# A hand-ordered decoder layer: four stage joins rearranged (squares and tables, GLA to NSA, the first decode batch, the output weights)

## The chip, the cores and the metric

One core of a Trainium2 chip runs the whole program. The time is device microseconds of one execution. The kernel before was timed in three runs, and one more execution of it was profiled.

## The reference

One decoder layer in fp32 works on 512 prompt tokens and on 32 sample tokens (8 sequences of 4 new tokens, each behind 4,096 cached ones), with D = 1024 and the same weights for both groups. Cut to what matters:

```python
mod = silu(c) @ w_ada + b_ada                    # six modulation vectors
u = x * (1 + sc1) + sh1                          # x: LayerNorm of the input
z = u @ w_in                                     # split into GLA and NSA columns
o_g = gated linear attention(q_g, k_g, v_g, a_g) # 4 heads, chunks of 64, RMSNorm, swish gate
o_n = nsa(q_n, kv_c, kv_s, kv_w, gates)          # 8 heads, 2 kv heads
x = LN(ALPHA * x + ga1 * (concat(o_g, o_n) @ w_o))
x = LN(ALPHA * x + ga2 * ((silu(gate) * up) @ w_ffn_out))   # gate, up from w_ffn_in
```

NSA sums three attentions with sigmoid gates. One goes over compressed keys and values: every 32 tokens, with a stride of 16, go through a small MLP (`cmp_w1`, gelu, `cmp_w2`). One goes over the 16 blocks of 64 tokens with the highest scores, and one over a window of 512 tokens. For the sample group, the cached rows of the compress branch, of the selected branch and of the window come from HBM.

## The kernel before, in words

The program is written by hand: each of the five engines (PE = TensorE, DVE = VectorE, ACT = ScalarE, POOL = GpSimd, SP, which only issues transfers) has one list of instructions, in the order of the text, and named semaphores join the lists. No scheduler moves anything. An engine that waits holds up everything behind the wait on its list.

The stages, with their times in the profile: LayerNorm and the modulation weights (0 to 50 us); the input projection (50 to 216); GLA (216 to 288); the NSA prompt loop of 32 tiles (288 to 386); eight decode batches, one for each sample sequence (386 to 658); output projection and LayerNorm (658 to 757); the feed-forward part and the last LayerNorm (757 to the end).

Large buffers are shared by the stages. `ring` (the profile's ringreg) has four slots of 1 MB, through which all weights pass, and in decode the selected rows. `RC` (creg) holds U early on, and the compress rows of the even decode batches; `RS` (sreg) holds the squares early on and the compress rows of the odd batches. `Z` (zreg) holds the projection, `XC` and `MIXT` (mixreg) the centred rows and later the attention outputs.

**Head.** DVE writes the centred rows of the LayerNorm (L1907). ACT squares them (`ln_act`, L1514), PE sums the squares. Ahead of the squares ACT waits for all constant tables (`consts_in`), among them the page table `ptc`. PE multiplies the tiles of `w_ada` as they come; tiles 5 to 8 are asked for by SP (L393) as PE frees slots (`weights_used`). DVE waits for the tables ahead of `fold_gain`.

**GLA to NSA.** DVE scales the GLA outputs, first the sample's and then four banks (L2142, L2144). PE transposes heads 0, 2, 1, 3 into banks 4, 5, 0, 1 (L1089) and then the sample's (L1093). DVE multiplies each by its gate into MIXT (L2149, L2152) and then copies the swapped keys (`kswap`, L2162), and POOL copies the swapped queries (L636). PE waits for all of that and computes `scores(0)` into banks of the first two transposes. The loop of 32 tiles then runs on all engines. DVE makes the scaled sample queries zS (L2193) ahead of the loop; the transfers of SP that copy them wait for that.

**Decode batches.** For one batch POOL gathers eight pieces of compress rows (`cmp_load`, L646, 0.5 MB each, into RC or RS) and the selected rows (`slc_load`, L652, 4 MB, into ring). DVE transposes the pieces (`turn_in`, L2199) and the selected keys (L2229). POOL adds pairs (`pair_sums_of`, L667), PE multiplies pieces and sums by `cmp_w1` (`outer`, `inner`), DVE adds the hidden rows up (`hidden_in`, L2236 to L2239), ACT and POOL compute the gelu (`gelu_cubic` L672, `gelu_product` L677), PE makes the compressed keys (`cmp_keys`) and values (`cmp_values`) from it. Then come scores, importance, choice of blocks (DVE, L2257 on), masks, exponentials and values. Each batch's last steps run under the next batch's first. Batch 0 has a code path of its own in many places: `weight_sum(1)` (POOL, L658) prepares the second weight sum that `cmp_w1` needs, and `cmp_load(1)` is issued in two groups of four among batch 0's pair sums.

**Output weights.** SP, in its order, loads the window rows and two pieces of VX for each batch (L458 to L460), then waits until the last batch's values and scores have left the ring, and asks for the four tiles of `w_o` (L382). PE runs `wo_tile(n, h)` (eight column tiles, n, and two halves of the tokens, h), with pieces of the last batch (`cmp_values(7)` and its tail) between them. The late modulation weights (`ada_load`, L469) follow into the slots that the output tiles free.

## Time and profile before

| | |
|---|---|
| three runs | 1202.77, 1206.3, 1208.32 us (median 1206.3) |
| profiled execution | 1201.1 us, its span 1199.3 us |
| mean granted TensorE clock | 0.963 of full speed |
| PE busy | 1123.1 us, 94% of the span |
| DVE busy | 690.5 us, 58% |
| ACT busy | 332.5 us, 28% |
| POOL busy | 304.8 us, 25% |
| HBM read, written | 158.84 MB, 9.24 MB |

The busy time of an engine is an average over stages with different limits, so the places that count are found in the timeline. A timeline row has the start of an instruction or of a run of equal ones, its length, the engine, the line and operation, output <- inputs, shapes, how many, and in brackets the idle time before it with what ended it. A count of x4 with one length means that four instructions took that length together.

### The profile page before, as it was taken

Reading aid. Unit: us, or ns where it says so; the run is one execution under the profiler, and the core shown is the slowest. Engines: PE = TensorE matmul, PEld = TensorE weight load, DVE = VectorE, ACT = ScalarE, POOL = GpSimd, SP = SyncE. Lnnn points to the kernel's source line nnn. Section 1 sums busy time; section 2 is a strip of 40 time slices with the busy share of each in tenths; the row PEclk is TensorE's granted clock in tenths of the full one; section 3 lists DMA queues with packets and bytes.
Section 4 is the critical chain, followed back from the end, with each engine's and each line's share of the span. In section 5 each row is a group of like instructions: output and inputs, shape, how many; then the busy total and the mean of one; then the engine's idle time right before and its main releaser. Section 6 shows DMA issues by size and latency. Waiting matters only on the chain.

```text
span 1199.3 us, 19658 instructions
## 1 busy us (share of the span) xinstructions
PE 1123.1 (94%) x7798; PEld 885.4 (74%) x7798; DVE 690.5 (58%) x1496; ACT 332.5 (28%) x783; POOL 304.8 (25%) x346
## 2 busy tenths in 40 slices
PE   5899999877999799999999899999999999999995
PEld 3577777654677577877777686788887888778884
DVE  2753332688777478877775446554455454563245
ACT  2111110624665244544454213221111111000005
POOL 7200000163535677666662001000010000000000
PEclk8899999877999899999999999999999999999998
DMA  7733332155400776666663316121221221320202
GB/s 292 281 141 140 146 153 94 36 196 141 119 2 8 292 298 277 248 249 258 238 246 141 141 37 241 60 84 71 94 81 70 75 99 48 145 90 12 93 1 75
DMA packets 36842, 165.33 MB, mean 138 GB/s; under 512 B 4968, under 2 KB 15816, under 8 KB 27608
## 3 DMA queue, kind: packets, MB, share of 16 engines
q1 hardware_dynamic: 25304, 94.78, 21.5%
q0 software_dynamic: 11312, 69.38, 14.9%
q8 instruction: 56, 0.92, 0.3%
q14 instruction: 26, 0.21, 0.1%
q10 hardware_dynamic: 144, 0.04, 0.0%
HBM read 158.84 MB, written 9.24 MB: 140 GB/s over the span
## 4 chain that ended last, share of the span: by engine, by line
PE 83%; DVE 6%; DMA 4%; ACT 2%; POOL 2%; issue 1%; SPq 0%; ACTq 0%; DVEq 0%; POOLq 0%
PE PS L366 82%; DMA VX<-out_dram 2%; DMA ptc<-in_ptab_dram 1%; PE PS L1182 1%; POOL ptc L519 1%; ACT trunk L1829 1%; DVE w L2407 1%; DMA ringreg<-in_w_ada_dram 1%; DVE sreg L2455 1%; DVE sreg L2090 0%; DVE creg L2090 0%; PE PS L1255 0%; ACT ringreg L1643 0%; DMA ringreg<-in_w_o_dram 0%; DVE ringreg L2115 0%
## 5 line engine op out<-in xcount | busy, mean ns | idle before, releaser
L366 PE MATMUL PS<-mixreg,w 128*128 128x272 f32 (+1 forms) x596 | 139.7, 386 | 9.9 <-DVE mixreg L2085 4.2
L366 PE MATMUL PS<-creg,ringreg 128*128 128x272 f32 (+1 forms) x564 | 144.2, 400 | 3.5 <-ACT creg L1522 2.8
L366 PE MATMUL PS<-mixreg,ringreg 128*128 128x272 f32 (+1 forms) x532 | 132.3, 402 | 5.5 <-DMA ringreg<-in_w_o_dram 4.4
L366 PEld LDWEIGHTS PS<-mixreg,w 128*128 128x128 f32 x596 | 110.5, 195 | 32.0 <-issue 8.3
L366 PEld LDWEIGHTS PS<-creg,ringreg 128*128 128x128 f32 (+1 forms) x564 | 104.6, 188 | 33.1 <-issue 9.8
L366 PEld LDWEIGHTS PS<-mixreg,ringreg 128*128 128x128 f32 (+1 forms) x532 | 100.2, 191 | 28.0 <-DMA ringreg<-in_w_o_dram 4.8
L366 PE MATMUL PS<-zreg 128*32 128x128 f32 (+4 forms) x832 | 107.2, 327 | 9.1 <-POOL zreg L667 4.8
L366 PE MATMUL PS<-creg,w 128*128 128x256 f32 (+1 forms) x432 | 106.7, 392 | 0.0
L366 PEld LDWEIGHTS PS<-creg,w 128*128 128x128 f32 x432 | 81.8, 193 | 17.6 <-issue 4.3
L366 PEld LDWEIGHTS PS<-zreg 128*32 128x32 f32 (+2 forms) x832 | 73.0, 142 | 23.0 <-issue 6.0
L366 PE MATMUL PS<-mixreg,sreg 128*128 128x272 f32 x352 | 87.3, 395 | 0.0
L366 PEld LDWEIGHTS PS<-mixreg,sreg 128*128 128x128 f32 x352 | 66.1, 190 | 13.1 <-issue 0.2
L366 PE MATMUL PS<-sreg,w 128*128 128x256 f32 x256 | 61.6, 386 | 0.0
L366 PE MATMUL PS<-sreg,ringreg 128*128 128x128 f32 (+2 forms) x488 | 55.2, 309 | 1.3 <-DVE sreg L2096 0.7
L366 PEld LDWEIGHTS PS<-sreg,ringreg 128*128 128x128 f32 (+2 forms) x488 | 46.9, 189 | 11.5 <-issue 7.8
L366 PEld LDWEIGHTS PS<-sreg,w 128*128 128x128 f32 x256 | 47.1, 190 | 10.0 <-issue 4.5
L685 POOL TENSOR_SCALAR sreg<-ident,ringreg 128x128 f32<-128x128 f32 x64 | 37.8, 602 | 46.6 <-DVE ringreg L2183 46.6
L667 POOL TENSOR_TENSOR zreg<-sreg 128x512 f32<-128x512 f32 x32 | 40.0, 1277 | 30.3 <-DVE sreg L2199 30.0
L366 PE MATMUL PS<-zreg,sreg 128*128 128x272 f32 (+1 forms) x192 | 44.0, 448 | 1.2 <-ACT zreg L1615 1.2
L667 POOL TENSOR_TENSOR zreg<-creg 128x512 f32<-128x512 f32 x32 | 40.1, 1277 | 19.5 <-DVE creg L2199 18.8
L594 POOL MEMSET sreg<- 128x512 f32 x1 | 0.5, 519 | 166.1 <-DVE mod L1891 166.1
L740 POOL TENSOR_TENSOR sreg<-zreg 128x2992 f32<-128x2992 f32 x1 | 6.5, 6544 | 142.1 <-DVE zreg L2438 142.1
(392 smaller groups left out, 1873.7 us busy)
## 6 DMA issues: line engine op xcount, KB each, us to landing
ringreg<-in_w_ada_dram SPq DMA_DIRECT2D x24, 1024.0 KB, 7.1
ringreg<-in_w_f_dram SPq DMA_DIRECT2D x22, 1024.0 KB, 4.8
ringreg<-in_w_in_dram SPq DMA_DIRECT2D x11, 1024.0 KB, 4.8
ringreg<-in_w_f_dram SPq DMA_DIRECT2D x8, 704.0 KB, 4.2
creg<-in_w_f_dram SPq DMA_DIRECT2D x8, 704.0 KB, 6.8
sreg<-in_win_dram SPq DMA_DIRECT2D x8, 512.0 KB
ringreg<-in_w_o_dram SPq DMA_DIRECT2D x4, 1024.0 KB, 8.0
out_dram<-in_win_dram SPq DMA_DIRECT2D x1, 4064.0 KB
```

What stands on the lines that cost most here:

```text
L366: return nc.tensor.matmul(o, lhsT, rhs, start=start, stop=stop, **kw)
L519: pool.dma_start(ptc[i * 32:(i + 1) * 32, s, :], a["ptab"][8 * s:8 * s + 8, :].unsqueeze(1).to_broadcast([8, 4, DB])).then_inc(sem("consts ...
L594: nc.gpsimd.memset(pcp, 0.0).then_inc(sem("pcp"), 1)
L667: nc.gpsimd.tensor_tensor(row_sums(n).rearrange("p (x s n) -> p x s n", x=4, s=4), x[:, 0], x[:, 1], ALU.add).then_inc(sem("seg_sum"), 1)
L685: nc.gpsimd.tensor_scalar(DG[t % 2][:, q, :], ident[:, :], pst[:, t % 2, 3, q:q + 1], None, ALU.mult).then_inc(sem("nsa_p"), 1)
L740: nc.gpsimd.tensor_tensor(T2[0], HB[0][1], HB[0][0], ALU.subtract).then_inc(sem("u_s"), 1)
L1182: last = nc.tensor.transpose(PS[:, pt_banks[n // 4], (n % 4) * P:(n % 4 + 1) * P], PSC[:, c:c + P], ident[:, :])
L1829: nc.scalar.activation(X[:, k, t], XC[:, k, t], ACT.Identity, bias=lnv[:, 5, k:k + 1], scale=lnv[:, 4, k:k + 1]).then_inc(sem("ln_x"), 1)
L2407: nc.vector.tensor_tensor(o, x, y, op).then_inc(sem("blk_s"), 1)
L2455: nc.vector.tensor_tensor(o, x, y, op).then_inc(sem("blk_s"), 1)
```

## The change

The diff below is cut to its core; semaphore counts that merely follow a new order are in it where PE waits on them.

- Head: ACT's squares go ahead of the wait for the tables, and DVE's wait for them goes from `fold_gain` up to the seventh `ada_row`, the first reader.
- GLA to NSA: the banks are scaled, transposed and multiplied in the order in which the scores need them; the sample's part comes last; `scores(0)` waits for two MIXT products in place of five, the first `values` for five; `kswap` goes from DVE to ACT; the four zS scalings go into turns 2 to 5 of the loop.
- First batch: `weight_sum(1)` goes ahead of `slc_load(0)`; the eight `cmp_load(1)` are spread among the sums and the gelu steps; `outer(0, 6)` goes ahead of `cmp_keys(0)`; `turn_in(0, 7)` ahead of `hidden_in(0, 0)`.
- Output weights: tiles 0 and 1 go into the upper half of RC, asked for when the last pair sum and piece have been multiplied; tiles 2 and 3 stay in ring slots 2 and 3. The first two `ada_load` wait for output tiles 1 and 3 in place of 10 and 12.

```diff
+        wo_slot = [RC[:, 4096:4096 + SLOT], RC[:, 4096 + SLOT:4096 + 2 * SLOT], ring[2], ring[3]]
...
+            sp.wait_ge(sem("cmp_mm"), NX * (DB - 1))
+            for k in range(2):
+                sp.dma_start(wo_slot[k], a["w_o"][k]).then_inc(sem(f"ring_full{k}"), 16)
             sp.wait_ge(sem("v_copy"), 4 * DB)
             sp.wait_ge(sem("sc_s"), DB)
-            stretch(a["w_o"], S_O, N_O, ring)
+            for k in range(2, N_O):
+                sp.dma_start(wo_slot[k], a["w_o"][k]).then_inc(sem(f"ring_full{k}"), 16)
             def ada_load(k):
-                sp.wait_ge(sem("wo_tile"), KD + 2 * (k + 1))
+                sp.wait_ge(sem("wo_tile"), KD + 2 * (k + 1) if k >= 2 else 2 * k + 1)
...
+            weight_sum(1)
             pool.wait_ge(sem("zs"), 8)
             slc_load(0)
-            weight_sum(1)
             pair_sums_of(0, 2)
             pair_sums_of(0, 3)
-            cmp_load(1, range(4))
+            cmp_load(1, range(2))
             pair_sums_of(0, 4)
-            cmp_load(1, range(4, 8))
+            cmp_load(1, range(2, 3))
             pair_sums_of(0, 5)
+            pair_sums_of(0, 6)
             gelu_cubic(0, 0)
-            pair_sums_of(0, 6)
+            cmp_load(1, range(3, 4))
             gelu_product(0, 0)
+            cmp_load(1, range(4, 6))
             pair_sums_of(0, 7)
+            cmp_load(1, range(6, 8))
...
-            for n, h in enumerate((0, 2, 1, 3)):
-                pe.wait_ge(sem("gla_on"), 2 + 2 * (n // 2) + 1)
+            for n, h in enumerate((1, 3, 0, 2)):
+                pe.wait_ge(sem("gla_on"), 2 * (n // 2) + 2)
...
-            pe.wait_ge(sem("gla_done"), 1)
+            pe.wait_ge(sem("gla_on"), 5)
+            pe.wait_ge(sem("gla_done"), 3)
             nc.tensor.transpose(PS[:, 4, 0:P], ON[:, 16, :], ident[:, :]).then_inc(sem("gla_mt"), 1)
...
             pe.wait_ge(sem("nsa_co"), R)
-            pe.wait_ge(sem("gla_done"), GH + 1)
+            pe.wait_ge(sem("gla_done"), 2)
             pe.wait_ge(sem("nsa_q"), 4)
             pe.wait_ge(sem("nsa_ks"), 2)
             scores(0)
...
                         if b:
                             tail_values(b - 1)
+                        else:
+                            outer(b, 4 * c + 2)
                         cmp_keys(b)
-                    outer(b, 4 * c + 2)
+                    if b or c == 0:
+                        outer(b, 4 * c + 2)
                     inner(b, 4 * c + 2)
...
+            ln_act(0)
             act.wait_ge(sem("consts_in"), 144 + 256)
-            ln_act(0)
...
+            for g in range(G):
+                nc.scalar.activation(kswap[HD - g * HD:P - g * HD], Z[g * HD:(g + 1) * HD, ZKV + 4, 0:LP], ACT.Copy).then_inc(sem("nsa_ks"), 1)
...
+            dve.wait_ge(sem("consts_in"), 144 + 256)
             for k in range(6, N_ADA1):
                 ada_row(k, k, 6)
...
-            dve.wait_ge(sem("consts_in"), 144 + 256)
             fold_gain(0, 0, 0)
...
-            for g in range(G):
-                nc.vector.tensor_copy(kswap[HD - g * HD:P - g * HD], Z[g * HD:(g + 1) * HD, ZKV + 4, 0:LP]).then_inc(sem("nsa_ks"), 1)
...
+                if 2 <= t < 2 + R:
+                    nc.vector.tensor_scalar(zS[:, t - 2, :], Z[:, ZQN + t - 2, LP:NT], HD ** -0.5, None, ALU.mult).then_inc(sem("zs"), 1)
...
+                if b == 0:
+                    turn_in(b, 7)
                 hidden_in(b, 0)
-                turn_in(b, 7)
+                if b:
+                    turn_in(b, 7)
```

ACT in the head, before (sreg<-mixreg are the squares, creg<-trunk,mod the first rows of U; line numbers of the changed kernel are some higher):

```order
L1532 ACTIVATE sreg<-sreg 128x72 [waits c_in]
L1514 ACTIVATE sreg<-mixreg 128x544 [waits ln_cent,consts_in]
L1514 ACTIVATE sreg<-mixreg 128x544 [waits ln_cent] x7
L1516 ACT_TABLE_LOAD
L1516 ACTIVATE rstd<-rstd 128x136 [waits ln_rec]
L1522 ACTIVATE creg<-trunk,mod 128x512 [waits ln_h,mod_one]
```

and in the changed kernel:

```order
L1547 ACTIVATE sreg<-sreg 128x72 [waits c_in]
L1529 ACTIVATE sreg<-mixreg 128x544 [waits ln_cent] x8
L1531 ACT_TABLE_LOAD
L1531 ACTIVATE rstd<-rstd 128x136 [waits ln_rec]
L1537 ACTIVATE creg<-trunk,mod 128x512 [waits ln_h,mod_one,consts_in]
```

The wait for the tables has moved from the first square to the first row of U.

POOL in the first decode batch, before (sreg<-in_cmp_dram are the gathers for batch 1, zreg<-creg pair sums, zreg<-w the weight sum, zreg<-zreg,hxs the gelu's steps):

```order
L652 DMA ringreg<-in_slc_dram,idx 128x8192 [waits zs]
L658 TENSOR_TENSOR zreg<-w 128x1024
L667 TENSOR_TENSOR zreg<-creg 128x512 [waits seg_t] x2
L646 DMA sreg<-in_cmp_dram,idxc 128x1024 x4
L667 TENSOR_TENSOR zreg<-creg 128x512 [waits cmp_mm,seg_t]
L646 DMA sreg<-in_cmp_dram,idxc 128x1024 x4
L667 TENSOR_TENSOR zreg<-creg 128x512 [waits cmp_mm,seg_t]
L672 TENSOR_TENSOR zreg<-zreg,hxs 128x512 [waits cmp_sq]
L667 TENSOR_TENSOR zreg<-creg 128x512 [waits cmp_mm,seg_t]
L677 TENSOR_TENSOR zreg<-zreg,hxs 128x512 [waits cmp_tanh]
L667 TENSOR_TENSOR zreg<-creg 128x512 [waits cmp_mm,seg_t]
```

and in the changed kernel:

```order
L664 TENSOR_TENSOR zreg<-w 128x1024
L658 DMA ringreg<-in_slc_dram,idx 128x8192 [waits zs]
L673 TENSOR_TENSOR zreg<-creg 128x512 [waits seg_t] x2
L652 DMA sreg<-in_cmp_dram,idxc 128x1024 x2
L673 TENSOR_TENSOR zreg<-creg 128x512 [waits cmp_mm,seg_t]
L652 DMA sreg<-in_cmp_dram,idxc 128x1024
L673 TENSOR_TENSOR zreg<-creg 128x512 [waits cmp_mm,seg_t] x2
L678 TENSOR_TENSOR zreg<-zreg,hxs 128x512 [waits cmp_sq]
L652 DMA sreg<-in_cmp_dram,idxc 128x1024
L683 TENSOR_TENSOR zreg<-zreg,hxs 128x512 [waits cmp_tanh]
L652 DMA sreg<-in_cmp_dram,idxc 128x1024 x2
L673 TENSOR_TENSOR zreg<-creg 128x512 [waits cmp_mm,seg_t]
L652 DMA sreg<-in_cmp_dram,idxc 128x1024 x2
```

Sums 5 and 6 and the gelu's first step now stand ahead of five of the gathers, and the last gather stands behind sum 7.

SP at the end of decode, before (VX<-out_dram are the last pieces of batch 7):

```order
L460 DMA VX<-out_dram 4x128
L378 UNCONDITIONAL_BRANCH [waits sc_s,v_copy]
L382 DMA ringreg<-in_w_o_dram 128x2048 [waits weights_used] x4
L378 REGISTER_ALU
L378 COMPARE_AND_BRANCH
L469 DMA ringreg<-in_w_ada_dram 128x2048 [waits wo_tile] x2
```

and in the changed kernel:

```order
L462 DMA VX<-out_dram 4x128
L466 DMA creg<-in_w_o_dram 128x2048 [waits cmp_mm]
L466 DMA creg<-in_w_o_dram 128x2048
L470 DMA ringreg<-in_w_o_dram 128x2048 [waits sc_s,v_copy]
L470 DMA ringreg<-in_w_o_dram 128x2048
L475 DMA ringreg<-in_w_ada_dram 128x2048 [waits wo_tile] x2
```

Two of the four loads now stand ahead of the wait for the last scores and values, and go into creg.

## Rows read from the trace of the kernel before

**Rows 1.** The page: busy time, share of the span and instructions of each engine.
```profile
PE 1123.1 (94%) x7798; PEld 885.4 (74%) x7798; DVE 690.5 (58%) x1496; ACT 332.5 (28%) x783; POOL 304.8 (25%) x346
```

**Rows 2.** PE's waits: what waited <- releaser: us idle, times, mean us.
```profile
PE PS L366 <- ACT sreg L1514: 6.9, 1, 6.9
```

**Rows 3.** Timeline, 0 to 55: start us, us busy, engine, line, operation, count [idle before <-releaser].
```profile
13.98 5.14 DVE L1907 TENSOR_TENSOR mixreg<-trunk,PS 128x544 f32<-128x544 f32 x8 [8.29 <-PE PS L366]
15.01 17.69 SPq L393 DMA_DIRECT2D ringreg<-in_w_ada_dram  x4
...
16.46 1.07 PE L366 MATMUL PS<-ringreg,cs 128*32 128x256 f32 x16 [1.52 <-DMA ringreg<-in_w_ada_dram]
...
23.75 4.49 ACT L1514 ACTIVATE sreg<-mixreg 128x544 f32<-128x544 f32 x8 [18.57 <-DMA ptc<-in_ptab_dram]
...
39.04 1.94 PE L366 MATMUL PS<-ringreg,cs 128*32 128x256 f32 x16 [1.49 <-DMA ringreg<-in_w_ada_dram]
...
45.59 3.72 PE L366 MATMUL PS<-creg,ringreg 128*128 128x272 f32 x8 [2.80 <-ACT creg L1522]
```

**Rows 4.** Windows: length, busy of PE, PEld, DVE, ACT, POOL, granted clock, DMA share, GB/s.
```profile
2.00:24.00 22.00, 11.19 (x64) 7.93 (x64) 6.58 (x15) 1.04 (x3) 19.25 (x57) 0.87 0.98 371
22.00:24.00 2.00, 0.00 (x0) 0.00 (x0) 0.00 (x0) 0.24 (x1) 1.35 (x7) 0.50 1.00 414
403.00:414.00 11.00, 5.84 (x14) 3.67 (x15) 4.62 (x4) 3.53 (x5) 7.91 (x7) 0.54 0.81 327
```

**Rows 5.** Timeline, 268 to 300, the join of GLA and NSA.
```profile
282.89 3.05 DVE L2149 SCALAR_TENSOR_TENSOR mixreg<-PS,gng,creg 128x512 f32<-128x512 f32 x4
...
286.23 1.40 DVE L2162 COPY ringreg<-zreg 64x512 f32<-64x512 f32 x2
...
287.78 0.48 PE L366 MATMUL PS<-zreg 64*128 64x128 f32 x1 [2.70 <-DVE ringreg L2162]
```

**Rows 6.** Timeline, 376 to 436, the first decode batch.
```profile
388.19 1.00 POOL L652 DMA_INDIRECT ringreg<-in_slc_dram,idx  x1 [2.17 <-DVE grow L2309]
...
398.96 0.42 DVE L2239 TENSOR_TENSOR hxs<-hxs,PS 128x256 f32<-128x256 f32 x1
...
403.57 4.62 DVE L2229 STREAM_TRANSPOSE ringreg<-ringreg 128x1024 f32<-128x1024 f32 x4 [3.04 <-DMA ringreg<-in_slc_dram,idx]
404.07 0.93 POOL L646 DMA_INDIRECT sreg<-in_cmp_dram,idxc  x1 [0.30 <-issue]
...
406.35 2.08 PE L366 MATMUL PS<-zreg 128*128 128x256 f32 x4 [4.79 <-POOL zreg L667]
...
417.61 4.60 DVE L2199 STREAM_TRANSPOSE sreg<-sreg 128x1024 f32<-128x1024 f32 x4
...
423.07 0.42 DVE L2236 TENSOR_TENSOR hxs<-PS,hxs 128x254 f32<-128x254 f32 x1 [0.86 <-ACT hxs L1677]
...
432.32 3.50 DVE L2199 STREAM_TRANSPOSE sreg<-sreg 128x1024 f32<-128x1024 f32 x3
...
434.67 1.95 PE L366 MATMUL PS<-sreg,w 128*128 128x256 f32 x8
```

**Rows 7.** Timeline, 632 to 690, the end of decode and the output weights.
```profile
648.51 0.29 SPq L460 DMA_DIRECT2D VX<-out_dram  x1
...
658.68 2.09 SPq L382 DMA_DIRECT2D ringreg<-in_w_o_dram  x4
...
662.26 0.42 DVE L2239 TENSOR_TENSOR hxs<-hxs,PS 128x256 f32<-128x256 f32 x1
...
663.58 9.14 PE L366 MATMUL PS<-mixreg,ringreg 128*128 128x272 f32 x32 [4.45 <-DMA ringreg<-in_w_o_dram]
...
666.75 1.27 POOL L677 TENSOR_TENSOR zreg<-zreg,hxs 128x512 f32<-128x512 f32 x1 [1.40 <-ACT zreg L1692]
...
672.56 1.00 PE L366 MATMUL PS<-w,zreg 128*128 128x64 f32 x8
...
673.40 3.88 PE L366 MATMUL PS<-mixreg,ringreg 128*128 128x272 f32 x16
```

More of the change, by code:

```diff
@@ L1084, in _ @@
                 last.then_inc(sem("nsa_cv"), 1)
-            for n, h in enumerate((0, 2, 1, 3)):
-                pe.wait_ge(sem("gla_on"), 2 + 2 * (n // 2) + 1)
+            for n, h in enumerate((1, 3, 0, 2)):
+                pe.wait_ge(sem("gla_on"), 2 * (n // 2) + 2)
                 for t in range(TT):
-                    last = nc.tensor.transpose(PS[:, (4, 5, 0, 1)[n], t * P:(t + 1) * P],
+                    last = nc.tensor.transpose(PS[:, (0, 1, 4, 5)[n], t * P:(t + 1) * P],
                                                ON[:, 4 * (2 * (h % 2) + t // 2) + 2 * (t % 2) + h // 2, :], ident[:, :])
                 last.then_inc(sem("gla_mt"), 1)
-            pe.wait_ge(sem("gla_done"), 1)
+            pe.wait_ge(sem("gla_on"), 5)
+            pe.wait_ge(sem("gla_done"), 3)
             nc.tensor.transpose(PS[:, 4, 0:P], ON[:, 16, :], ident[:, :]).then_inc(sem("gla_mt"), 1)
@@ L1145, in values @@
                     pe.wait_ge(sem("nsa_out"), t)
+                elif t == 0:
+                    pe.wait_ge(sem("gla_done"), GH + 1)
                 for k in range(j + 1):
@@ L1318, in wo_tile @@
                 for c in range(KD):
-                    last = matmul(PS[:, bank, 0:HALF], wslot[(S_O + n // 2) % RING][:, c, n % 2 * P:(n % 2 + 1) * P],
+                    last = matmul(PS[:, bank, 0:HALF], wo_slot[n // 2].rearrange("p (k c) -> p k c", k=KD)[:, c, n % 2 * P:(n % 2 + 1) * P],
                                   MIXT[:, c, h * HALF:(h + 1) * HALF], c == 0, c == KD - 1)
@@ L2141, in _ @@
             dve.wait_ge(sem("gla_rstd"), 1)
-            nc.vector.tensor_scalar(ON[:, 16, :], ON[:, 16, :], gms[:, 16:17], None, ALU.mult).then_inc(sem("gla_on"), 1)
-            for n in range(4):
+            for n in (2, 3, 0, 1):
                 nc.vector.tensor_tensor(ON[:, 4 * n:4 * n + 4, :], PS[:, (4, 5, 0, 1)[n], :].rearrange("p (n v) -> p n v", n=4),
                                         gms[:, 4 * n:4 * n + 4].unsqueeze(2).to_broadcast([P, 4, P]), ALU.mult).then_inc(sem("gla_on"), 1)
+            nc.vector.tensor_scalar(ON[:, 16, :], ON[:, 16, :], gms[:, 16:17], None, ALU.mult).then_inc(sem("gla_on"), 1)
             dve.wait_ge(sem("gla_tm"), 2)
-            for n, h in enumerate((0, 2, 1, 3)):
+            for n, h in enumerate((1, 3, 0, 2)):
                 dve.wait_ge(sem("gla_mt"), n + 1)
-                nc.vector.scalar_tensor_tensor(out=MIXT[:, h, 0:LP], in0=PS[:, (4, 5, 0, 1)[n], :], scalar=gng[:, 0:1], in1=TH[:, h, 0:LP],
+                nc.vector.scalar_tensor_tensor(out=MIXT[:, h, 0:LP], in0=PS[:, (0, 1, 4, 5)[n], :], scalar=gng[:, 0:1], in1=TH[:, h, 0:LP],
                                                op0=ALU.mult, op1=ALU.mult).then_inc(sem("gla_done"), 1)
@@ L2190, in output @@
                 nc.vector.tensor_tensor(o, o, PS[HD - g * HD:P - g * HD, 4 + g, 0:P], ALU.add).then_inc(sem("nsa_out"), 1)
-            for r in range(R):
-                nc.vector.tensor_scalar(zS[:, r, :], Z[:, ZQN + r, LP:NT], HD ** -0.5, None, ALU.mult).then_inc(sem("zs"), 1)
             def turn_in(b, k):
```

## Prediction

> **What bounds the kernel now.** I read the page first, then PE's list of waits, then the timeline and windows around the waits that the change touches. TensorE (PE) is busy 1123.1 of 1199.3 us [rows 1]. So the kernel is a chain of PE work with a few holes, and a change is worth what it takes out of the holes, or out of PE work done at the lower of its two clocks (granted clock 0.5 is 1.2 GHz, 1.0 is 2.4 GHz). The reader is to see four holes: 6.9 us in the head for ACT's squares [rows 2], 2.70 for the two key copies at the join [rows 5], 4.79 for a pair sum of POOL in the first batch [rows 6], 4.45 for the first output weights [rows 7]. From about 50 to 216 us (input projection) and in the feed-forward stages after 757 us PE finds its operands ready, so whatever is gained ahead of them is simply carried along.
>
> The sum is made against the profiled execution, 1201.1 us (span 1199.3 and 1.8 around it). The median of the three runs is 1206.3, 0.4% above it; the forecast takes the same microseconds off the median. A measurement of this kernel can tell about 0.5%, 6 us, from no change.
>
> **Head: −7.0.** ACT's eight squares stood behind the wait for the tables: they began at 23.75 after 18.57 idle and ended at 28.24 [rows 3]. Their operands, DVE's centred rows, were written from 13.98 to 19.12. Freed, the last square ends one square (4.49/8 = 0.6) behind the last row, at 19.7: 8.5 earlier, the upper bound. But the modulation weights then come into it. SP asks for tiles 5 to 8 of w_ada as slots come free, and its four issues reach from 15.01 to 32.7, because PE, stuck at the squares, was late to free them [rows 3]. Now PE frees them sooner and the transfers follow each other. PE saw tile 2 at 16.46 and began tile 8 at 39.04. A tile is 1.05 MB: at the 414 GB/s of the window 22 to 24 it takes 2.53 us, at the mean of 2 to 24, 371 GB/s, 2.83 [rows 4]. I take 2.6, near the first, since the tables that shared the queue until 23.75 are then in. Tile 8 comes at 16.46 + 6 × 2.6 = 32.0 instead of 39.04, 7.0 earlier; at the mean rate 33.4, 5.6 earlier, the lower bound. Behind tile 8 nothing changes: 6.55 us to the first block product at 45.59 [rows 3] (row turn, fold, U), which becomes 38.6. The wait for the tables moves down to where they are first read; they are in at 23.75, before either engine gets there, so it costs nothing; if they came 5 us later it would still stand under the weight tiles.
>
> The Trainium skill, "DMA: Bandwidth & Descriptors", section "Where 436 GB/s comes from", says that between HBM and SBUF the HBM side, some 358 GB/s for one core, is what binds. By it a tile takes 2.93 us, tile 8 comes at 34.0, and the head's term is −5.0 instead of −7.0. The 414 GB/s row does not agree with it, and the measurement decides.
>
> **GLA to NSA: −2.0.** Before, PE stood 2.70 us before scores(0) at 287.78, for DVE's two kswap copies (286.23, 1.40), and these stood behind four MIXT products (282.89 to 285.94, 0.76 each) and the sample one [rows 5]. Now ACT makes the copies, behind its own evacuations and beside DVE's products: hidden. DVE's third product (282.89 + 3 × 0.76 = 285.2) [rows 5] is late next: it frees the bank for the sample transpose, which PE has ahead of scores(0). So scores(0) comes at about 285.55, 2.2 sooner. The scores' banks are those whose products are now first, so they do not wait for the other two. The four zS scalings, a sixteenth of the width of a kswap copy of 0.70, go into loop turns 2 to 5; I allow 0.2 for them. The loads that wait for them are needed a hundred microseconds later. I take −2.0, bounds 0 (DVE, not PE, sets the loop's pace and was ready anyway) to −2.5.
>
> **First batch: −5.2.** Before, POOL issued eight gathers of compressed rows (cmp_load) in two blocks of four; each costs 0.93 and 0.30 to the next, and the last went at 404.07 [rows 6]. Behind them stood pair sum 5, for which PE waited 4.79; its next four products took 2.08 us, and over 403 to 414 the granted clock was 0.54 [rows 4, 6]: the 5.84 us that PE worked there hold about 5.84 × 0.46 = 2.7 of slow clock. Now sums 5 and 6 and the cubic come ahead of the last five gathers. DVE's hidden rows are done at 399.38 [rows 6]; in batch 7 the product began 4.07 after them (662.68 to 666.75) [rows 7], so here it runs from 403.4 to 404.65. PE has outer(0,6) ahead of the keys, so it does not wait for that: no hole over 1 us is left, and the clock should stay at 1.0. The price is the last gather. Behind the product stand two gathers, sum 7, two gathers: 404.65 + 2 × 1.25 + 1.28 + 0.1 + 1.25 puts the last issue at 409.8, 5.7 later than before. slc_load moves behind weight_sum(1), which now fills POOL's 2.17 idle: 388.45 for 388.19 [rows 6], so the four key transposes begin at 403.85.
>
> What counts is then when the last gather lands, L, since DVE's turn_ins of batch 1 need it. A half-megabyte gather should land no later after its issue than the one-megabyte output tile, 4.9 us (658.68 to 663.58) [rows 7], so at 414.7; I take L = 414.4. From L on: before, DVE's first turn_in began at 417.61 and PE's outer(1,4) at 434.67, 17.06 later, of which 0.86 was idle for ACT and 1.15 PE's own delay after the turn_in (432.32 + 1.2 = 433.5) [rows 6]: 15.05 of work. outer(1,4) at 414.4 + 15.05 = 429.45, 5.2 sooner. Bounds: L = 413 (3.2 us behind the issue) gives −6.6; L = 417.75 (8 us behind it, which is how long after the old last issue the queue was still emptying: 0.81 of 403 to 414) [rows 4] gives −1.9. Moving turn_in(0,7) ahead of the hidden rows costs them 1.2 us at most, covered by outer(0,6).
>
> **Output weights: −4.5.** Before, w_o was asked for at 658.68, when the last batch's scores had left the ring; PE was free at 659.13 and waited until 663.58, and 32 products then took 9.14 us where 16 later took 3.88, 1.4 more than full speed [rows 7]. Now tiles 0 and 1 go to the upper half of the compressed-row buffer, free once the last pair sum is multiplied, and SP reaches them behind batch 7's VX at 648.51 + 0.29 [rows 7]: 2 MB in 10 us on a queue with little else. wo_tile(0) runs from 659.13 to 663.0, tile 1 to 666.9, both at full clock. Then a **new wait** shows: cmp_values(7) needs POOL's gelu product, which ends at 666.75 + 1.27 = 668.02 [rows 7] whatever PE does. So cmp_values begins at 668.05 instead of 672.56: −4.5. Without the new wait it would be −6.0 (upper bound: 672.56 − 666.9 and a little); −2.5 if the queue of SP is late or the clock falls in the wait. Tiles 2 and 3 are asked for as before and needed 15 us later: free. The ada loads no longer reuse slots of w_o and go sooner, into an idle queue.
>
> **Sum:** 7.0 + 2.0 + 5.2 + 4.5 = 18.7. 1206.3 − 18.7 = **1187.6** (profiled execution 1182.4). The lower bounds add up to 10.0, the upper to 23.6.
>
> **The rivals.**
> Tiles at the mean rate. The weights, not the squares, set the head; for it: 371 GB/s over 22 us [rows 4]; against: that stretch holds the small tables. Head −5.6: 1189.0. The skill's rule named above is this case at a little lower rate, and would give 1189.6.
> Late gathers. Moved 5.7 us down, the last gathers land when DVE already waits, and the batch's gain is given back: for it, the later issue; against, the DMA share of 0.81 over 403 to 414 [rows 4] says that the queue was emptying. With none left: 1192.8.
> Clock. The short new waits (key transposes in batch 0, POOL's product at w_o) let the clock fall to 1.2 GHz as in 403 to 414; 2.7 + 1.4 of gain go: 1191.7.
> More. No new wait at w_o and L early: 1.5 + 1.4 more, 1184.7.
> Slower. Loads for batch 1 that end later make each later batch's loads later, and DVE's turn_in waits in every batch. A batch takes (663.58 − 388.19)/8 = 34.4 us and moves 8 × 0.52 + 4.2 + 0.5 = 8.9 MB, 21.6 us at 414 GB/s, so 12.8 are spare and the lag should be gone after one batch. To be slower by 6 us it would have to cost (18.7 + 6)/7 = 3.5 us in each of seven batches: 1212.3.
> That the change does not do what it says: the instruction order shows each move, so this has no chance of its own.
>
> **How the numbers follow.** Forecast 0.58; mean-rate tiles 0.09; late gathers 0.13; clock 0.07; more 0.04; several terms missing at once, with 6 us or less left of the gain, 0.04; slower 0.05. The first five are faster by over 0.5%: 0.91; the sixth is within, 0.04; the last slower, 0.05. All lower bounds together give 1196.3, all upper ones 1182.7; with some spread of the runs the range is 1181 to 1197. It leaves out the last two cases.
>
> **What would show it.** Right: squares beginning near 14.6; the first block product near 38.6; no wait of PE for the squares; scores(0) 2.2 us sooner against the stage before; no PE hole over 1 us from 400 to 415 and a clock of 1.0 there; DVE's first turn_in of batch 1 waiting for a DMA; no PE wait for w_o and one of about 1.15 for POOL's product. Wrong: a PE wait for w_ada that has grown by more than 3 us, a clock near 0.5 in 403 to 414, DVE waits for gathers in batch after batch, or cmp_values no sooner after batch 7 than before.

## The result, and the profile after

The changed kernel takes 1188.33 us (median of 4 runs, 1186.29 to 1188.71) against 1204.73 of the kernel before: a ratio of 0.9864, with a 95% interval of 0.9839 to 0.9888. That is 16.4 us less (13.5 to 19.4). The forecast was 1187.6, in a range of 1181 to 1197. Two later comparisons of the same change gave 0.9886 (0.9864 to 0.9908) and 0.9863 (0.9837 to 0.9889).

The profiled execution of the changed kernel took 1188.67 us with a span of 1186.9, 12.4 less than the profiled execution before. The runs show more, since the profiled execution of before, 1201.1, lies at the low end of that kernel's runs (1200.4 to 1209.1 over all comparisons); what varies in it is in the last section.

The page after, busy time by engine (answers to [rows 1]):

```profile
PE 1124.2 (95%) x7798; PEld 884.9 (75%) x7798; DVE 687.7 (58%) x1494; ACT 334.9 (28%) x785; POOL 305.5 (26%) x346
```

PE does the same work as before; what has gone is idle time. PE's waits after (what waited <- releaser: us idle in all, times, the longest one; the third number is the longest in [rows 2], too, not the mean):

```profile
PE PS L1267 <- DMA VX<-out_dram: 4.3, 6, 1.9
...
PE PS L368 <- DVE ringreg L2244: 2.9, 1, 2.9
...
PE PS L368 <- POOL zreg L683: 2.0, 2, 1.4
...
PE PS L368 <- DMA ringreg<-in_w_ada_dram: 1.6, 3, 0.9
...
PE PS L368 <- ACT sreg L1529: 1.0, 5, 0.2
```

The 6.9 us for ACT's squares [rows 2] are 1.0, and the waits for pair sum 5, the key copies and `w_o` [rows 5 to 7] are off the list. New are 2.9 for the selected keys (L2244) and 1.4 for the last gelu product (L683), and the wait for the window load, put down to VX, has grown; before, it was 2.5 for six, the longest 0.6.

The head after, timeline (answers to [rows 3]):

```profile
14.71 5.14 DVE L1924 TENSOR_TENSOR mixreg<-trunk,PS 128x544 f32<-128x544 f32 x8 [9.07 <-PE PS L368]
15.46 5.08 ACT L1529 ACTIVATE sreg<-mixreg 128x544 f32<-128x544 f32 x8 [10.33 <-DVE mixreg L1924]
...
15.73 9.22 SPq L395 DMA_DIRECT2D ringreg<-in_w_ada_dram  x4
...
29.69 1.74 PE L368 MATMUL PS<-ringreg,cs 128*32 128x256 f32 x16 [0.87 <-DMA ringreg<-in_w_ada_dram]
...
32.31 1.94 PE L368 MATMUL PS<-ringreg,cs 128*32 128x256 f32 x16
...
39.00 3.97 PE L368 MATMUL PS<-creg,ringreg 128*128 128x272 f32 x8 [2.94 <-ACT creg L1537]
```

The squares run right behind the centred rows, SP's four tiles are asked for in 9.2 us and not 17.7, tile 8 begins at 32.31 (before 39.04) and the first block product at 39.00 (before 45.59). From here to the low-rank gate product (zM), behind the input projection, the two executions take the same time: 172.2 us (before 172.0). The window 20 to 40 (columns as in [rows 4]):

```profile
20.00:40.00 20.00, 15.45 (x154) 9.57 (x155) 13.20 (x27) 4.10 (x6) 8.43 (x27) 0.75 1.01 416
```

The weights come at 416 GB/s over 20 us. The Trainium skill, "DMA: Bandwidth & Descriptors", section "Where 436 GB/s comes from", lets the HBM side bind at some 358 GB/s; the trace does not agree with it, and the measurement decides. The same section also holds a measured 16 MB load at 425 GB/s, and that one the trace comes near to.

The join after (answers to [rows 5]):

```profile
275.98 1.28 ACT L1637 ACTIVATE ringreg<-zreg 64x512 f32<-64x512 f32 x2
...
276.63 3.22 DVE L2166 SCALAR_TENSOR_TENSOR mixreg<-PS,gng,creg 128x512 f32<-128x512 f32 x4
...
279.73 0.34 PE L368 MATMUL PS<-zreg 64*128 64x128 f32 x1 [0.29 <-POOL ringreg L642]
```

ACT copies the swapped keys beside DVE's products; scores(0) begins 3.1 us after the first of these (279.73 against 276.63) where it was 4.9 before (287.78 against 282.89).

Batches 0 and 1 after (answers to [rows 6]):

```profile
380.36 1.00 POOL L658 DMA_INDIRECT ringreg<-in_slc_dram,idx  x1 [0.40 <-DVE grow L2324]
...
397.43 4.63 DVE L2244 STREAM_TRANSPOSE ringreg<-ringreg 128x1024 f32<-128x1024 f32 x4 [6.41 <-DMA ringreg<-in_slc_dram,idx]
...
401.43 0.94 POOL L652 DMA_INDIRECT sreg<-in_cmp_dram,idxc  x1 [0.30 <-issue]
...
402.11 4.08 PE L368 MATMUL PS<-ringreg,zreg 32*32 32x256 f32 x128 [2.86 <-DVE ringreg L2244]
...
407.27 4.62 DVE L2212 STREAM_TRANSPOSE sreg<-sreg 128x1024 f32<-128x1024 f32 x4 [3.77 <-DMA sreg<-in_cmp_dram,idxc]
...
413.71 0.95 POOL L658 DMA_INDIRECT ringreg<-in_slc_dram,idx  x1
...
422.72 1.97 PE L368 MATMUL PS<-sreg,w 128*128 128x256 f32 x8 [1.04 <-DVE sreg L2212]
...
439.26 0.89 PE L1267 MATMUL PS<-ident,sreg 128*128 128x128 f32 x4 [1.86 <-DMA VX<-out_dram]
...
440.08 3.96 PE L368 MATMUL PS<-ringreg,zreg 32*32 32x256 f32 x128
```

The last gather is asked for at 401.43 and has landed at 407.27, where DVE had waited for it for 3.77 us. The next selected rows are asked for at 413.71, behind POOL's four pair sums of batch 1. At 439.26 PE waits 1.86 us for batch 1's window load, and the block scores behind it take 3.96 us, where batches 2 to 7 take 2.75. The same place in the kernel before:

```profile
449.92 0.66 PE L1255 MATMUL PS<-ident,sreg 128*128 128x128 f32 x4 [0.59 <-DMA VX<-out_dram]
450.51 2.76 PE L366 MATMUL PS<-ringreg,zreg 32*32 32x256 f32 x128
```

The granted clock (the last number but two) over the two slow block scores, and the DMA share (the last number but one) over the 18 us that begin 42 us behind the end of the prompt loop, all in the changed kernel (windows, columns as in [rows 4]):

```profile
402.00:406.00 4.00, 3.89 (x128) 2.63 (x128) 0.84 (x4) 2.93 (x5) 0.37 (x1) 0.57 0.86 299
440.00:444.00 4.00, 4.00 (x130) 2.57 (x129) 3.53 (x4) 2.49 (x3) 3.75 (x3) 0.63 0.01 4
420.20:438.20 18.00, 16.15 (x150) 12.58 (x149) 13.45 (x25) 9.49 (x23) 12.89 (x12) 1.00 0.96 391
```

The transfers are full (0.96) nearly until the window load lands. They are as full in the kernel before (0.99 over the same 18 us), but there PE comes to this place 2.3 us later, counted from the end of the loop, and waits 0.59.

The output weights after (answers to [rows 7]):

```profile
640.06 0.83 SPq L466 DMA_DIRECT2D creg<-in_w_o_dram  x2
...
650.28 7.62 PE L368 MATMUL PS<-mixreg,creg 128*128 128x272 f32 x32
...
657.99 1.26 POOL L683 TENSOR_TENSOR zreg<-zreg,hxs 128x512 f32<-128x512 f32 x1 [1.40 <-ACT zreg L1709]
...
659.30 1.10 PE L368 MATMUL PS<-w,zreg 128*128 128x64 f32 x8 [1.40 <-POOL zreg L683]
```

Both tiles are there when PE is free, 32 products take 7.62 and not 9.14 us, and then PE waits 1.40 for POOL's product: the forecast new wait of 1.15. (The upper half of RC, into which they go, was free in time: its last user is batch 6.)

### The profile page after: what moved, and what is told of

It is laid out like the page before. It is cut to its first block, busy times and chain, and to the rows that moved or that the text cites. A ratio compares the mean times of both kernels' runs of the same rounds, so it can differ in the third digit from the quotient of the medians.

```text
span 1186.9 us, 19655 instructions
## 1 busy us (share of the span) xinstructions
PE 1124.2 (95%) x7798; PEld 884.9 (75%) x7798; DVE 687.7 (58%) x1494; ACT 334.9 (28%) x785; POOL 305.5 (26%) x346
## 3 DMA queue, kind: packets, MB, share of 16 engines
q0 software_dynamic: 11312, 69.38, 15.1%
## 4 chain that ended last, share of the span: by engine, by line
PE 84%; DVE 6%; DMA 4%; ACT 3%; issue 2%; POOL 1%; SPq 0%; ACTq 0%; DVEq 0%; POOLq 0%
PE PS L368 82%; DMA VX<-out_dram 2%; PE PS L1194 1%; ACT trunk L1846 1%; DMA ringreg<-in_w_ada_dram 1%; DVE w L2425 1%; DVE sreg L2212 0%; DMA sreg<-in_cmp_dram,idxc 0%; DVE creg L2107 0%; ACT sreg L1529 0%; ACT ringreg L1660 0%; PE PS L1267 0%; DMA out_dram<-ringreg 0%; POOL sreg L691 0%; ACT creg L1582 0%
## 5 line engine op out<-in xcount | busy, mean ns | idle before, releaser
L368 PE MATMUL PS<-mixreg,ringreg 128*128 128x272 f32 (+1 forms) x404 | 100.4, 400 | 1.0 <-DVE sreg L2443 1.0
L368 PEld LDWEIGHTS PS<-mixreg,ringreg 128*128 128x128 f32 (+1 forms) x404 | 75.0, 188 | 18.0 <-DVE sreg L2443 1.5
```

What stands on the lines that cost most here:

```text
L368: return nc.tensor.matmul(o, lhsT, rhs, start=start, stop=stop, **kw)
```

## The experiments

Theory A is the forecast: four terms that stand by themselves and add up. Theory B came from the trace above: three terms stand, but the first batch's gain is given back in batch 1, where PE waits for the window load and runs at the lower clock. Each kernel was compared with the kernel before on the same chip: the first four with 1204.17 us (29 runs), the next four with 1203.14 (11), the last four with 1204.5 (11). Since 2 us can hardly be told from nothing by the time, the stages of all profiled executions stand in a table behind the runs.

**The head alone.** ACT's squares ahead of the wait, DVE's wait moved.

```diff
+            ln_act(0)
             act.wait_ge(sem("consts_in"), 144 + 256)
-            ln_act(0)
```

> The head alone: squares ahead of the wait for the tables, all else as before. Theory A (the forecast's terms stand by themselves and add up): first block product about 7.0 us sooner (45.59 to 38.6), the whole 7 us faster. Theory B (the parts stand, but the first batch's gain is given back in the second) says the same here; the trace of the full change shows 6.6. If the gain were shortened by slower weight tiles it would be 5.6 or less.

Measured: 1198.13 us, 0.9952 (0.9933 to 0.9971), 5.8 us faster (3.5 to 8.1). The first block product, timeline:

```profile
39.09 3.51 PE L366 MATMUL PS<-creg,ringreg 128*128 128x272 f32 x7 [2.52 <-ACT creg L1522]
```

6.5 us sooner than in the execution before. Both theories hold.

**The join alone.** All hunks of the join.

```diff
-            pe.wait_ge(sem("gla_done"), GH + 1)
+            pe.wait_ge(sem("gla_done"), 2)
```

> The GLA to NSA join alone. Theory A: scores(0) 2.2 us sooner and 2.0 us off the whole. Theory B the same; the trace of the full change shows 1.8 at the end of the prompt loop. A third view, that DVE's zS scalings in the loop take the gain back, says 1.5 or less at the end of the loop while scores(0) is 2.2 sooner.

Measured: 1202.42 us, 0.9984 (0.9966 to 1.0003), 1.9 us faster (0.4 slower to 4.1 faster). By the time alone this is inconclusive. In its profiled execution scores(0) comes 5.59 us after ACT's last step of the GLA norm (`gms`, L1617 in the kernel before), where the four executions with the old join take 7.67 to 8.09: 2.3 less than their mean, as both theories say. The prompt loop behind it takes 98.3 us for 98.8, so the third view, that the scalings take the gain back, falls.

**The first batch alone.** The orders of POOL, PE and DVE there.

```diff
-            cmp_load(1, range(4))
+            cmp_load(1, range(2))
             pair_sums_of(0, 4)
-            cmp_load(1, range(4, 8))
+            cmp_load(1, range(2, 3))
             pair_sums_of(0, 5)
```

> The first decode batch's order alone. Theory A: outer(1,4) 5.2 us sooner (429.5 for 434.67) and 5.2 off the whole. Theory B: outer(1,4) 3 to 4 us sooner, but the last batch's transposes of the window only 0 to 1 us sooner, since in batch 1 PE waits about 2 us for the window load and runs 4 us or so at the lower clock; the whole 0 to 1 us faster.

Measured: 1205.56 us, 1.0006 (0.9988 to 1.0024): 0.7 slower (2.9 slower to 1.4 faster). Theory A's 5.2 is out. The timeline around the last gather:

```profile
419.89 4.62 DVE L2205 STREAM_TRANSPOSE sreg<-sreg 128x1024 f32<-128x1024 f32 x4 [4.93 <-DMA sreg<-in_cmp_dram,idxc]
...
435.34 3.15 PE L366 MATMUL PS<-sreg,w 128*128 128x256 f32 x8 [1.67 <-DVE sreg L2205]
```

DVE waits 4.93 us for the gathers, PE 1.67 for the transposes ahead of outer(1,4), and these eight products then take 3.15 us where eight at full clock take 1.97: outer(1,4) is 3.9 sooner behind the end of the prompt loop than before (44.16 for 48.06), and 2.3 of it is left at cmp_values(6) (247.38 for 249.66) and at the last batch's window transposes. So theory B has the 3 to 4 right, but not the 0 to 1 behind it, and not its reason here: in this execution the wait for the window load is 0.23 us and batch 1's block scores take 2.76. That the whole is no faster comes in part from the head, which is the old one and took 49.98 us in this execution (last section).

**The output weights alone.**

```diff
+            for k in range(2):
+                sp.dma_start(wo_slot[k], a["w_o"][k]).then_inc(sem(f"ring_full{k}"), 16)
             sp.wait_ge(sem("v_copy"), 4 * DB)
```

> The output weights alone. Theory A: no wait for w_o, a wait of about 1.15 us (by the full change's trace 1.40) for POOL's gelu product ahead of cmp_values(7), and 4.5 us off there and off the whole. Theory B the same. If the early loads delayed batch 7's own loads, cmp_values(7) would gain under 3 us.

Measured: 1201.43 us, 0.9966 (0.9952 to 0.9981), 4.1 us faster (2.3 to 5.8). The end of decode, timeline:

```profile
659.12 7.61 PE L368 MATMUL PS<-mixreg,creg 128*128 128x272 f32 x32
...
668.13 1.10 PE L368 MATMUL PS<-w,zreg 128*128 128x64 f32 x8 [1.41 <-POOL zreg L683]
669.07 5.57 PE L368 MATMUL PS<-mixreg,creg 128*128 128x272 f32 x16
```

As forecast: full speed of the first two tiles, and a wait of 1.41 for POOL's product (L683). Not forecast in the sum is what follows: the third tile takes 5.57 us where it took 3.88 before [rows 7], so the clock fell behind the new wait.

The four times add up to 11.1 us, with an interval of some 4 either way (the four half-widths, 2.3, 2.2, 2.2 and 1.7, squared, added and the root taken); that is 6.9 to 15.3. Of the whole change's three measurements, 13.7, 16.4 and 16.5, it takes in the first; the intervals of the others (13.4 to 19.6 together) overlap it. So the times do not contradict that the parts add up, and do not show it either; the stages below do that better.

**The change without the first batch's part.** Head, join and output weights stay; POOL's, PE's and DVE's order of batch 0 is the old one.

```diff
-            cmp_load(1, range(2))
+            cmp_load(1, range(4))
             pair_sums_of(0, 4)
-            cmp_load(1, range(2, 3))
+            cmp_load(1, range(4, 8))
```

> The full change without the first batch's new order (head, join and output weights stay). Theory A (the first batch is worth 5.2 us): 5 us slower than the full change. Theory B (its gain is given back in batch 1): 0.5 to 2.5 us slower; outer(1,4) 3.5 us later behind the end of the prompt loop than in the full change, cmp_values(6) 0.5 to 2.5 later.

**The change again**, with no edit, beside it:

> The full change as it is, again, beside the others on this chip: 1186 to 1189 us. Both theories say the same; its trace shows how far the head and batch 1 differ from one profiled execution to the next.

Measured: 1188.05 us without the part (0.9882, 0.9862 to 0.9903), 1188.73 with it (0.9886, 0.9864 to 0.9908). Theory A's 5 us are not there; by the medians what there is lies below theory B's 0.5, too, but the spread of six runs each leaves some 2 us either way (an estimate). In the two profiled executions outer(1,4) is 2.2 later without the part (3.5 expected) and cmp_values(6) is 1.0 sooner. Without the part the old hole is back (PE's waits):

```profile
PE PS L368 <- POOL zreg L673: 4.8, 1, 4.8
```

So a hole of 4.8 us that was read rightly was closed, and the time can't tell the gain from nothing; by the stage table it is 1.1.

**The selected rows asked for sooner.** If batch 1's transfers start too late, asking sooner must bring the gain back.

```diff
-                for k in range(XR):
-                    pair_sums_of(b, k)
+                pair_sums_of(b, 0)
                 pool.wait_ge(sem("v_copy"), 4 * b)
                 pool.wait_ge(sem("sc_s"), b)
                 slc_load(b)
+                for k in range(1, XR):
+                    pair_sums_of(b, k)
```

> The full change, with the selected rows of batches 1 to 7 asked for behind the first pair sum of the batch and not behind the fourth. Theory B says that batch 1 loses its gain because its loads start late (413.7 us) and the transfers are saturated until the window load lands: the request should come about 3.8 us sooner, PE's wait for batch 1's window load (1.9 us) should go, and cmp_values(1) to (6) come 1 to 4 us sooner. Theory A (gathers are not the limit) says no change, within 0.5 us.

**The same, and batch 0's block scores last.**

```diff
-                        block_scores(b)
+                        if b:
+                            block_scores(b)
                     outer(b, 4 * c + 3)
                     inner(b, 4 * c + 3)
+                    if c and b == 0:
+                        block_scores(b)
```

> As the last, and PE makes outer(0,7) and inner(0,7) ahead of the block scores of batch 0, which wait 2.9 us for the selected rows. Theory B: that wait goes, the clock stays at 1.0, but the first transposes of batch 1 still wait for the last gather, so outer(1,4) comes 0 to 1 us sooner than in the last kernel; scores of batch 0 end 2 to 3 us sooner, so that the next selected rows are asked for sooner by as much. If PE's own work were the limit, outer(1,4) would come 3 us sooner.

Measured: 1195.77 us (0.9942, 0.992 to 0.9963) and 1196.22 (0.9944, 0.9923 to 0.9964): 7 us slower than the change. My edit was wrong for batches 2 to 7. There POOL reaches the wait before the scores are made, as this row of the first kernel's batch 3 shows:

```profile
481.30 0.95 POOL L658 DMA_INDIRECT ringreg<-in_slc_dram,idx  x1 [3.99 <-PE PS L368]
```

It stands 3.99 us, and three pair sums and the gelu of the batch before stand behind it; each of batches 2 to 6 lost 1.6 to 2.4 us. But to cmp_values(1) the two were 1.5 and 3.0 us ahead of the change's first profiled execution (78.73 and 77.31 behind the end of the loop, for 80.28; its other two took 81.36 and 78.75). So the request was moved in batch 1 alone:

```diff
                 for k in range(XR):
                     pair_sums_of(b, k)
+                    if k == (0 if b == 1 else XR - 1):
+                        pool.wait_ge(sem("v_copy"), 4 * b)
+                        pool.wait_ge(sem("sc_s"), b)
+                        slc_load(b)
```

> The full change, with the selected rows asked for behind the first pair sum in batch 1 alone; in the later batches, where that order made POOL wait 4 us for the scores and held up its other sums, the request stays behind the fourth. Theory B (batch 1's transfers start late and are saturated): the wait for batch 1's window load goes or halves, and from the end of the prompt loop to cmp_values(1) to (6) it is 1.5 to 2.5 us shorter than in the full change; whole 1.5 to 2.5 us faster. Theory A: no change.

with batch 0's block scores last as well:

> As the last, and outer(0,7), inner(0,7) ahead of batch 0's block scores. From the traces of the two kernels with the early request in all batches: from the end of the prompt loop to cmp_values(1) 1.4 us less than without this order; against the full change 3 to 4 us less there, and the whole 3 us faster.

and, on top of both, with another order at the output weights:

```diff
-            cmp_values(DB - 1)
             wo_tile(2, 0)
+            cmp_values(DB - 1)
...
-            value_rows(DB - 1)
             exponentials_of(DB - 1)
+            value_rows(DB - 1)
```

> As the last, and PE makes the third output tile ahead of cmp_values(7), ACT batch 7's exponentials ahead of its compressed values. The wait of 1.40 us for POOL's gelu product goes, and everything behind it comes 1.4 us sooner; if ACT's exponentials or the later evacuation of the values were the limit, PE would wait as long one step later.

beside the change itself:

> The full change again, beside the three others: 1186 to 1190 us, from which their gains are read.

Measured: 1185.66 us (0.985, 0.9824 to 0.9875), 1185.78 (0.984, 0.9813 to 0.9867), 1182.79 (0.982, 0.9794 to 0.9846), and the change 1188.63 (0.9863, 0.9837 to 0.9889). The first of these, timeline:

```profile
404.71 4.62 DVE L2213 STREAM_TRANSPOSE sreg<-sreg 128x1024 f32<-128x1024 f32 x4 [5.37 <-DMA sreg<-in_cmp_dram,idxc]
...
407.45 0.95 POOL L658 DMA_INDIRECT ringreg<-in_slc_dram,idx  x1
...
435.37 0.66 PE L1268 MATMUL PS<-ident,sreg 128*128 128x128 f32 x4 [0.55 <-DMA VX<-out_dram]
```

The request follows the last gather's landing by 2.74 us where it was 6.44 (413.71 − 407.27), PE's wait for the window load is 0.55 for 1.86, and batch 1's block scores take 2.75. The DMA share over the same 18 us is 0.79 for 0.96:

```profile
417.70:435.70 18.00, 15.81 (x150) 12.31 (x149) 13.37 (x24) 9.56 (x24) 12.82 (x12) 1.00 0.79 296
```

The kernel is 3.0 us faster than the change by the medians, which the spread of the runs hardly tells from nothing (some 2.7 either way, an estimate). The stage is clearer: from the loop's end to cmp_values(6) the three kernels with the early request in batch 1 take 246.10, 246.16 and 246.22, where four executions without it take 247.38 to 250.69 (mean 248.77). That is what theory B said: batch 1's transfers began too late for a PE that came sooner. The early request was not tried with the old order of batch 0, so it isn't shown how much of its gain belongs to the late gathers; there PE waits 0.59 for the window load and the clock holds, so less could be gained. Block scores last added next to nothing (0.1 us slower by the medians, 0.2 sooner at cmp_values(1), where I expected 1.4): the wait for the selected keys went, but the gathers still set the next step, and PE waited 2.58 for their transposes instead. With the early request in all batches the same order had outer(1,4) 1.5 sooner (44.06 for 45.57), and there the last gather had landed 1.5 sooner, too. The last kernel makes three tiles without a wait:

```profile
646.98 11.28 PE L368 MATMUL PS<-mixreg,creg 128*128 128x272 f32 x48
...
654.68 1.27 POOL L683 TENSOR_TENSOR zreg<-zreg,hxs 128x512 f32<-128x512 f32 x1 [1.40 <-ACT zreg L1713]
...
658.10 1.00 PE L368 MATMUL PS<-w,zreg 128*128 128x64 f32 x8
```

From cmp_values(6) to the end it takes 557.40 us for 559.71 in the kernel without the exchange, 2.3 less where 1.4 was expected. With the wait, the 16 products of the next tile behind it took 5.57 us (granted clock 0.76 over 656 to 663); without it, 16 such products take 3.91. So at the next LayerNorm, where PE reads `rstd`, it is 3.4 ahead, of which 1.1 is lost again further on. It has the lowest median of the study, 5.8 us under the change and 21.7 under the kernel before.

**The stages of all profiled executions.** The means of the stage's length in us without and with the part, and in brackets the shortest and longest and the number of executions. The kernels with the selected rows sooner are left out of the third and fourth line, those whose last stage differs out of the fifth and sixth.

| stage | without | with | gain | forecast |
|---|---|---|---|---|
| start to first block product (head) | 45.73 (42.12 to 49.98; 4) | 38.05 (36.26 to 39.23; 10) | 7.7 | 7.0 |
| low-rank gate product (L366, zM) to scores(0) (join) | 70.31 (70.11 to 70.57; 4) | 68.00 (66.41 to 69.38; 10) | 2.3 | 2.0 |
| loop's end to outer(1,4) (first batch) | 47.96 (47.70 to 48.23; 5) | 44.63 (44.16 to 45.57; 4) | 3.3 | 5.2 |
| loop's end to cmp_values(6) (first batch, batches 1 to 6) | 249.88 (249.65 to 250.16; 5) | 248.77 (247.38 to 250.69; 4) | 1.1 | 5.2 |
| cmp_values(6) to cmp_values(7) (output weights) | 37.23 (36.29 to 37.69; 4) | 31.80 (31.79 to 31.81; 7) | 5.4 | 4.5 |
| cmp_values(6) to the end | 564.63 (563.07 to 565.26; 4) | 559.65 (559.44 to 559.80; 7) | 5.0 | 4.5 |

Line 2 takes in all of GLA, which the change does not touch; from ACT's last step of the GLA norm to scores(0) it is 7.88 (7.67 to 8.09; 4) and 5.85 (5.59 to 6.44; 10), 2.0 less. The prompt loop itself has a mean of 98.8 both ways, so the zS scalings in it show no cost. In line 4 the ranges overlap: its 1.1 rests on four executions that lie 3.3 us apart. The gain falls to that in batch 1 alone, since at cmp_values(1) the means are 80.88 and 79.74 already. Line 5 ends ahead of the products that the fallen clock slows, so line 6 is the better measure of the output weights. The gains of lines 1, 2, 4 and 6 make 16.1, beside the 16.4 of the time.

## Why the prediction was right, point by point

**The head** came as worked out: the squares bound, then the weight tiles. Tile 8 was forecast at 32.0 and began at 32.31, with waits of under 0.9 us for tiles ahead of it. The first block product, forecast for 38.6, came at 36.26 to 39.23 in ten executions. The forecast carried the 6.55 us behind tile 8 along as they were in the execution before, in which tile 8 itself ran at 1.2 GHz (1.94 for 1.07); where the clock held, they were 4.1 (32.16 to 36.26 in the second kernel with the rows sooner). So the mean gain is 7.7 for 7.0. By the 358 GB/s of the section of the Trainium skill named above, tile 8 would have come at 34.0 (an estimate from that figure); in ten executions it came at 32.06 to 33.37.

**The join** came as worked out: 2.0 to 2.3 by the stages for 2.0, and no cost of the scalings that shows (0.2 was allowed).

**The first batch** is the step that failed: "outer(1,4) at 414.4 + 15.05 = 429.45, 5.2 sooner", booked as 5.2 off the whole. Two things in it. The smaller one is L. POOL's last gather went out when it was forecast to, 23.19 us behind the loop's end, but it landed 5.84 us after its issue (401.43 to 407.27) where I took 4.6, and from there to outer(1,4) it was 15.45 us for 15.05; so the profiled execution had 3.6. In all nine executions with the new order, DVE's first turn_in comes 28.6 to 30.1 us behind the loop's end (forecast 27.8) and outer(1,4) 15.4 to 15.5 behind that, so L alone moves it; the mean gain is 3.3. The forecast also missed that the gathers, the first of them now asked for 3.7 us behind slc_load(0) and not 6.0, come in beside the selected rows, which took 17.1 us from issue to landing for 15.4 [rows 6]: PE waited 2.86 for the keys where no hole over 1 us was forecast, and the clock was down for the block scores (4.08 for 2.76). That did not delay outer(1,4), though, which follows L by the same time in the kernels without that wait.

The greater part is that I ended the term at outer(1,4) and put what follows in batch 1 at nothing. Batch 1's own transfers start behind POOL's pair sums, which wait for the late gathers; they then run until the window load lands, and the PE that came sooner waited for that. Between the two first profiled executions the gain goes from 3.6 us at outer(1,4) to 2.3 behind that wait (0.59 before, 1.86 after), to 0.9 at cmp_values(1), behind block scores at a fallen clock (2.76 before, 3.96 after), and to 0.4 at cmp_values(6). In the change's other two executions the wait is as long (1.85 and 1.95) and the block scores take 3.73 and 2.76. The prediction's 12.8 us of spare transfer time in a batch is a mean; ahead of this window load the transfers had next to none (0.96). In the sum the term should have been 1.1, the mean. The rival "late gathers" named the mechanism, with 0.13, and put it one batch too early.

**The output weights**: no wait for `w_o`, a new wait of 1.40 (forecast 1.15), and the first two tiles at full clock. The stage to cmp_values(7) is 31.80 in all executions that have it; before, it was 36.29 to 37.69, so the gain there is 5.4 for 4.5, since the one execution costed was the shortest of four. Behind the new wait the clock fell, as the rival "Clock" has it, in six of the seven executions of lines 5 and 6: the next 16 products took 5.57 us, and 3.89 only in the change's first profiled execution. To the end of the kernel it makes no difference that shows (559.45 in that one, 559.44 to 559.80 in the six), and the gain is 5.0; what gives the 1.7 us back further on was not looked for.

So the time was right in part by luck. The gain was 16.4 where 18.7 was forecast: the first batch fell short by 4.1, and the head, the join and the output weights gave 0.7, 0.3 and 0.5 more than the one profiled execution could show. And the kernel before ran at 1204.73 in this comparison, where the forecast started from 1206.3; this 1.6 brought 1188.33 to within 0.7 of the 1187.6. Of the rivals, the clock fell behind the new waits in most executions; nothing was slower in each of the later batches, so that rival fell: cmp_values(1) to cmp_values(6) took 168.97 us in the profiled execution and 168.53 before.

## What to carry to other kernels

In this kernel a hole of the bounding engine was worth its length only where what the engine met next was ready sooner too: follow the transfers of the next stage, and which instruction they are issued behind, before booking the gain. When an issue is moved ahead on an engine that runs in order, do it only where its wait has already been met there (in batch 1 it had, in the later ones POOL stood 4 us). And where a wait hangs on a clock or a transfer, cost it on several executions: the one that was profiled may be the shortest or the longest.

## What the runs showed of the hardware that was not expected

The same code had heads of 42.1 to 50.0 us before the change. In the execution of the first-batch kernel, whose head is the old one, the clock stayed low (windows):

```profile
29.00:50.00 21.00, 19.18 (x136) 11.09 (x136) 10.58 (x23) 1.52 (x4) 3.34 (x4) 0.50 0.77 288
```

PE had waited for the squares, and the granted clock was 0.50 over all of 29 to 50, so that each weight tile took 1.94 us; in the execution before, five tiles took 1.07 each at 2.4 GHz and the last 1.94. With the squares early PE waits less, and the ten heads lie within 3 us. The time's spread is smaller, too: 1200.4 to 1209.1 before (55 runs, standard deviation 2.6), 1185.7 to 1190.9 after (16 runs, 1.6). That the head is the reason is not shown.

The same in batch 1: two executions of the changed kernel waited alike for the window load, 1.86 and 1.95 us, and behind it the block scores took 3.96 in one (439.26, above) and 2.76 in the other:

```profile
441.18 0.66 PE L1267 MATMUL PS<-ident,sreg 128*128 128x128 f32 x4 [1.95 <-DMA VX<-out_dram]
...
441.76 2.76 PE L368 MATMUL PS<-ringreg,zreg 32*32 32x256 f32 x128
```

It is the same at the output weights: behind waits of 1.40 and 1.41 us the next tile took 3.9 us in three executions and 5.6 in six. Whether the clock falls behind a wait of this length isn't settled by the wait alone; what else decides was not tried.
